# Splitting a 16-chunk product of two norms and a projection 2, 4, 4, 6 instead of 4, 4, 4, 4

## The reference, cut to what matters

```python
mod = jax.nn.silu(c) @ w_mod + b_mod             # c: (1, 2048), w_mod: (2048, 3 * 2048)
shift, scale, gate = jnp.split(mod, 3, axis=-1)
h = rms_norm(x, g_pre) * (1.0 + scale[:, None, :]) + shift[:, None, :]
proj = h @ w_in                                  # (256, 2048) @ (2048, 5648)
...                                              # three mixers on slices of proj
y = jnp.concatenate([y_a, y_b, y_c], axis=-1) * jax.nn.silu(z)   # z: the last 2048 columns of proj
out = y @ w_out
return x + gate[:, None, :] * rms_norm(out, g_post)
```

## Time and profile before

| | |
|---|---|
| median of 3 runs | 2877.43 us (2876.9 to 2878.89) |
| the profiled execution, its own time | 2878.37 us |
| its span, first to last instruction | 2876.2 us |
| PE busy | 2807.3 us, 98% |
| DVE busy | 2162.3 us, 75% |
| ACT busy | 1518.5 us, 53% |
| DMA | 610.86 MB, mean 212 GB/s |

### The profile page before, as it was taken

One profiled execution on the slowest core, in us unless ns is written; L12 is line 12 of the kernel. 1 busy time (PEld: TensorE's weight loads), 2 busy tenths in 40 slices (PEclk: granted clock), 3 DMA queues, 4 the chain that ended last, 5 costly groups with the idle time before them and its releaser, 6 DMA issues.

```text
span 2876.2 us, 37268 instructions
## 1 busy us (share of the span) xinstructions
PE 2807.3 (98%) x14486; PEld 2416.6 (84%) x14486; DVE 2162.3 (75%) x2679; ACT 1518.5 (53%) x2108; POOL 42.7 (1%) x49
## 2 busy tenths in 40 slices
PE   7998998999999999999999999999999999999998
PEld 5886777898889888888888888898888888888887
DVE  8998998678855567666886678745676668866788
ACT  5455544665546555644554455565546445544554
POOL 0000000000000000000000000000000000000000
PEclk9999999999999999999999999999999999999999
DMA  9996597767745554555665566565545565555564
GB/s 394 369 373 227 184 361 301 273 205 249 247 157 174 162 169 154 172 189 195 199 205 183 191 197 199 188 191 162 169 154 172 188 196 199 205 183 191 197 214 160
DMA packets 173744, 610.86 MB, mean 212 GB/s; under 512 B 19665, under 2 KB 19937, under 8 KB 173057
## 3 DMA queue, kind: packets, MB, share of 16 engines
q1 hardware_dynamic: 170770, 599.38, 61.0%
q0 software_dynamic: 1824, 6.61, 0.8%
q10 hardware_dynamic: 976, 2.51, 0.3%
HBM read 606.30 MB, written 2.11 MB: 212 GB/s over the span
## 4 chain that ended last, share of the span: by engine, by line
PE 81%; DVE 3%; ACT 2%; issue 1%; DMA 1%; POOL 0%; SPq 0%; DVEq 0%; POOLq 0%; ACTq 0%
PE ps L2348 16%; PE ps L2279 15%; PE ps L2282 15%; PE ps L2286 14%; PE ps L2358 8%; PE ps L2221 2%; PE ps L2325 1%; PE ps L2327 1%; PE ps L2322 1%; PE ps L2558 1%; PE ps L2331 1%; PE ps L2336 1%; PE ps L2334 1%; DVE w_lo L1414 1%; DMA raw<-in_w_in 1%
## 5 line engine op out<-in xcount | busy, mean ns | idle before, releaser
L1414 DVE TENSOR_TENSOR w_lo<-raw,w_hi 128x1024 fp32r<-128x1024 f32 (+3 forms) x942 | 1088.8, 1176 | 505.2 <-ACT w_hi L1008 501.2
L1008 ACT ACTIVATE w_hi<-raw 128x1024 fp32r<-128x1024 f32 (+3 forms) x942 | 948.1, 1019 | 984.4 <-PE ps L2358 355.0
L2348 PE MATMUL ps<-hT_both,w_hi 128*128 128x512 f32 x2048 | 490.5, 391 | 1.1 <-DVE u L1570 0.9
L2279 PE MATMUL ps<-w_hi,hT_both 128*128 128x512 f32 (+3 forms) x1824 | 479.5, 384 | 7.9 <-DVE proj L1616 2.6
L2286 PE MATMUL ps<-w_hi,hT_both 128*128 128x512 f32 (+3 forms) x1824 | 458.9, 373 | 0.0
L2348 PEld LDWEIGHTS ps<-hT_both,w_hi 128*128 128x128 f32 x2048 | 376.0, 188 | 75.1 <-DVE u L1570 1.3
L2282 PE MATMUL ps<-w_lo,hT_both 128*128 128x512 f32 (+3 forms) x1640 | 414.7, 374 | 3.2 <-DVE w_lo L1414 3.2
L2286 PEld LDWEIGHTS ps<-w_hi,hT_both 128*128 128x128 f32 x1824 | 338.2, 188 | 48.6
L2279 PEld LDWEIGHTS ps<-w_hi,hT_both 128*128 128x128 f32 x1824 | 327.5, 190 | 54.6 <-DVE proj L1616 6.5
L2282 PEld LDWEIGHTS ps<-w_lo,hT_both 128*128 128x128 f32 x1640 | 305.0, 189 | 48.5 <-DVE w_lo L1414 5.0
L2358 PEld LDWEIGHTS ps<-hT_both,w_lo 128*128 128x128 f32 x2048 | 262.8, 191 | 10.2
(11 more groups left out here) (309 smaller groups left out, 2627.2 us busy)
## 6 DMA issues: line engine op xcount, KB each, us to landing
raw<-in_w_up SPq DMA_DIRECT2D x256, 512.0 KB, 3.7
raw<-in_w_down SPq DMA_DIRECT2D x256, 512.0 KB, 3.5
raw<-in_w_modT SPq DMA_DIRECT2D x162, 512.0 KB, 6.8
raw<-in_w_rest SPq DMA_DIRECT2D x80, 456.0 KB, 3.4
raw<-in_w_z SPq DMA_DIRECT2D x54, 512.0 KB, 4.3
raw<-in_w_out SPq DMA_DIRECT2D x49, 512.0 KB, 4.3
raw<-in_w_oa SPq DMA_DIRECT2D x32, 512.0 KB, 3.4
raw_more<-in_w_modT SPq DMA_DIRECT2D x30, 512.0 KB, 6.8
```

Of the source, the lines that this page charges most:

```text
L1008: act.activation(hi_blocks(L % SPLIT_SLOTS, c, w), blocks(raw_at(G), c, w), ACT.Copy).then_inc(S.hi_ready, 1)
L1414: dve.tensor_tensor(blocks(lo_at(G), c, w), blocks(raw_at(G), c, w), hi_blocks(s, c, w).bitcast(F32), ALU.subtract).then_inc(S.group_read, 1)
L2279: pe.matmul(o, rows(hi, c, t), wh[:, c], start=start and c == 0, stop=False)
L2348: pe.matmul(ps[:, bank(job, i, f)], wh[:, c, f * P:(f + 1) * P], hT_both[:, k0 + c].rearrange("p a n -> p (a n)"), start=k0 + c == 0, stop ...
```

## The change

The contraction of layer 0's input product is cut into parts of 2, 4, 4 and 6 chunks instead of four of 4. Layer 1 keeps one product with modulation columns in quarters. What follows from it:

- A has 8 steps (one group to a tile), B and C 16, D 24 (three groups to a tile). The sum stays 64 steps.
- 8 rows (4 pairs) are multiplied ahead of step 0 instead of 16. The 16 rows of B lie over the first 6 steps of A, the 16 of C over the first 13 of B, the 24 of D over the first 13 of C, and the 14 of the gate over the 24 steps of D.
- A has one lead, at step 0. B's two leads stand at steps 6 and 7, C's two at 22 and 23, D's three at 37, 38 and 39.
- DVE's add of a finished tile in D, the rotation and POOL's small loads are placed by steps that fit the longer D.

```diff
-QUARTERS = 4
-QC = KC // QUARTERS
+PORTIONS = (((0, 2), (2, 4), (6, 4), (10, 6)), ((0, 4), (4, 4), (8, 4), (12, 4)))
+FIRST_INPUT = ("ina", "inb", "inc", "ind")
...
-    for q in range(QUARTERS):
-        yield f"in{'abcd'[q]}0", "w_in", 0, q * QC, QC, 0, C_Z, C_Z // 8
+    for kind, (k0, cnt) in zip(FIRST_INPUT, PORTIONS[0]):
+        yield f"{kind}0", "w_in", 0, k0, cnt, 0, C_Z, C_Z // 8
...
-        mods_first = [mod_group(*m) for m in quarter_mods(0, 0)]
-        mods = [m for q in range(1, QUARTERS) for m in quarter_mods(0, q)] + gate_mods(0)
+        def portion_mods(l, q):
+
+            k0, cnt = PORTIONS[l][q]
+            return [(l, part * KC + k, h) for k in range(k0, k0 + cnt) for part in range(2) for h in range(2)]
+        mods_first = [mod_group(*m) for m in portion_mods(0, 0)]
+        mods = [m for q in range(1, len(PORTIONS[0])) for m in portion_mods(0, q)] + gate_mods(0)
...
-        parts = [(product(f"in{'abcd'[q]}0", hT, lhs0=q * QC, evac="dve" if q else "act", pinned=True),
-                  pace_pairs(16, 13) if q < QUARTERS - 1 else pace_pairs(14, 16)) for q in range(QUARTERS)]
+        parts = [(product(f"{kind}0", hT, lhs0=k0, evac="dve" if k0 else "act", pinned=True), times)
+                 for kind, (k0, _), times in zip(FIRST_INPUT, PORTIONS[0], (
+                     pace_pairs(16, 6), pace_pairs(16, 13), pace_pairs(24, 13), pace_pairs(14, 24)))]
...
-        lead("ina0", *after("ina0", 0), first=1)
...
-        for q, name in enumerate(("inb0", "inc0", "ind0")):
-            lead(name, *after(name, -2, -1), first=2 * q + 2)
+        for kind, (k0, cnt) in zip(FIRST_INPUT[1:], PORTIONS[0][1:]):
+            lead(f"{kind}0", *after(f"{kind}0", *range(-(cnt // 2), 0)), first=k0 // 2)
...
-                    walk.upto(jobs["ind0"].L + 9)
+                    walk.upto(last_in.L + 12)
                     rotation = rotation1(l)
                     next(rotation)
-                    walk.upto(jobs["ind0"].L + 11)
+                    walk.upto(last_in.L + 14)
```

More of the change, by code:

```diff
@@ L550, in build, with portion_of, portion_ends @@
         hT = (hT_hi, hT_lo)
-        def quarter_mods(l, q):
-            return [(l, part * KC + q * QC + k, h) for k in range(QC) for part in range(2) for h in range(2)]
+        def portion_mods(l, q):
+            k0, cnt = PORTIONS[l][q]
+            return [(l, part * KC + k, h) for k in range(k0, k0 + cnt) for part in range(2) for h in range(2)]
+        def portion_of(l, k):
+            return next(q for q, (k0, cnt) in enumerate(PORTIONS[l]) if k0 <= k < k0 + cnt)
+        def portion_ends(l, block):
+            return any(block == KC + k0 + cnt - 1 for k0, cnt in PORTIONS[l])
         def gate_mods(l):
             return [(l, 2 * KC + k, h) for k in range(KC) for h in range(2)]
-        mods_first = [mod_group(*m) for m in quarter_mods(0, 0)]
-        mods = [m for q in range(1, QUARTERS) for m in quarter_mods(0, q)] + gate_mods(0)
-        mods += [m for q in range(QUARTERS) for m in quarter_mods(1, q)] + gate_mods(1)
+        mods_first = [mod_group(*m) for m in portion_mods(0, 0)]
+        mods = [m for q in range(1, len(PORTIONS[0])) for m in portion_mods(0, q)] + gate_mods(0)
+        mods += [m for q in range(len(PORTIONS[1])) for m in portion_mods(1, q)] + gate_mods(1)
         shapes = {name: shape for name, *shape in weight_products()}
@@ L943, in _ @@
             rsqrt(2)
-            pool.wait_ge(S.group_multiplied, jobs["ind0"].L)
+            pool.wait_ge(S.group_multiplied, last_in.L + 8)
             for dst, src in ((cst[:, CONST_FIRST:], io["const"][:, CONST_FIRST:]), (cols2[:], io["cols2"]),
@@ L1068, in split_bank @@
                 if layer is not None:
-                    act.wait_ge(S.hcol_ready, QUARTERS * layer + 2 * b // QC + 1)
+                    act.wait_ge(S.hcol_ready, layer * len(PORTIONS[0]) + portion_of(layer, 2 * b) + 1)
                 u = n(S.lhs_hi) - 1
@@ L1163, in split @@
                 l = job.layer
-                if job.kind in ("ina", "inb", "inc", "ind", "in"):
+                if job.kind in (*FIRST_INPUT, "in"):
                     split_bank(hT_hi, b, hcol, mod[:, l], l)
@@ L1182, in wide @@
                 for job, i, j, L, splits in ahead(order):
-                    if prev and prev[0].kind == "ina" and j == 1:
+                    if prev and prev[0].kind == FIRST_INPUT[0] and j == len(job.groups[:2]) - 1:
                         evacuate(*prev)
@@ L1302, in mixers1 @@
                 if l == 0:
-                    d = jobs["ind0"]
+                    d = last_in
                     act.wait_ge(S.dve_evacuated, d.E + 6)
@@ L1611, in evacuate @@
                     return
-                if job.kind in ("inb", "inc", "ind"):
+                if job.kind in FIRST_INPUT[1:]:
                     if job.kind == "inb":
@@ L1646, in mod_product @@
                                          accum_out=mod_part[:, l, block, part:part + 1]).then_inc(S.group_read, 1)
-                if KC <= block < 2 * KC and block % QC == QC - 1 and part:
+                if part and portion_ends(l, block):
                     dve.wait_ge(S.group_read, G + 1)
-                    quarter_columns(l, (block - KC) // QC)
+                    portion_columns(l, block - KC)
             def mod_pair(l, block, part, G):
@@ L1658, in mod_pair @@
                                          accum_out=mod_part[:, l, block, 0:1]).then_inc(S.group_read, 2)
-                if KC <= block < 2 * KC and block % QC == QC - 1:
+                if portion_ends(l, block):
                     dve.wait_ge(S.group_read, G + 2)
-                    quarter_columns(l, (block - KC) // QC)
+                    portion_columns(l, block - KC)
             def side_by_side(G):
@@ L1675, in mod_products, with portion_columns @@
                         mod_product(*second)
-            def quarter_columns(l, q):
-                two = lambda v: v.rearrange("p (s k) -> p s k", s=2)[:, :, q * QC:(q + 1) * QC]
+            def portion_columns(l, last):
+                k0, cnt = PORTIONS[l][portion_of(l, last)]
+                k = slice(k0, k0 + cnt)
+                two = lambda v: v.rearrange("p (s k) -> p s k", s=2)[:, :, k]
                 m = two(mod[:, l, 0:2 * KC])
@@ L1683, in quarter_columns @@
                 link(dve.tensor_tensor(m, m, two(cols1[:, l, 16:16 + 2 * KC]), ALU.add))
-                k = slice(q * QC, (q + 1) * QC)
                 dve.scalar_tensor_tensor(out=hcol[:, k], in0=m[:, 1], scalar=1.0, in1=cols1[:, l, k],
@@ L1703, in wide @@
                         evacuate(*ended.pop(0)[0:2])
-                    if prev and prev[0].kind in ("inb", "inc", "ind") and j == 1:
+                    if prev and prev[0].kind in FIRST_INPUT[1:] and j == 1:
                         evacuate(*prev)
@@ L1879, in rotation1 @@
                 else:
-                    dve.wait_ge(S.dve_evacuated, jobs["ind0"].E + 3)
+                    dve.wait_ge(S.dve_evacuated, last_in.E + 3)
                 heads = QH + KVH
@@ L2266, in group_product @@
                 if pinned(job, i):
-                    start, stop = start and job.kind == "ina", stop and job.kind == "ind"
+                    start, stop = start and job.kind == FIRST_INPUT[0], stop and job.kind == FIRST_INPUT[-1]
                 terms = [(c, t, ps[:, bank(job, i, t), 0:job.width]) for c in range(cnt) for t in tokens]
@@ L2580, in gla @@
                 else:
-                    pe.wait_ge(S.dve_evacuated, jobs["ind0"].E + 7)
+                    pe.wait_ge(S.dve_evacuated, last_in.E + 7)
                 transposes([proj[:, t, C_CG:C_CG + RANK] for t in range(TOK)], RANK)
```

1 line of the change is left out of this document (added).

## The result

| | before | after |
|---|---|---|
| median | 2877.04 us (13 runs, 2875.02 to 2878.89) | 2884.02 us (13 runs, 2882.54 to 2888.27) |
| profiled execution, its span | 2876.2 us | 2882.2 us |
| time over that of before | | 1.0025, 95% interval 1.0017 to 1.0034 |

The change costs 6.98 us on the median; the forecast was 2884.4, 7.0 above its median. In the changed kernel `lo` is L1424, the pair L1666, the add L1626, the columns L1694 to L1696, the lead's subtraction L1768, and the three terms of a product L2290, L2293 and L2297.

What follows compares the result with a forecast made beforehand. DVE was taken to bound the kernel up to D's columns, PE behind them; D's end 7.3 us later less 0.3 past D gave 7.0 on the median 2877.43, 2884.4 us, range 2877.5 to 2890.

Steps and rivals of the forecast that it cites:

- The opening: Up to step 0's product: A's columns at 23.2, first product at 28.6 instead of 35.35, 6.7 us earlier.
- What the early start is worth: From 22.6 to D's columns: DVE idles 3.3 us instead of 5.7, a gain of 2.4 us.
- D's columns: The point where DVE forms D's columns, which fixes D: at 144.8 instead of 155.86.
- D: Last part, 24 steps: bound by PE at 2.44 us a product, takes 66.3 us, ends at 211.1, 7.3 us later.
- Past D: Behind D's end: DVE is less late for the first maxima, 0.3 of 1.1 us regained.
- the saving on DVE: Ahead of D's columns: 8 `lo` and one lead fewer on DVE, 8.1 and 0.6 us.
- PE is the bound: Rival, whole stage: PE keeps the 6.7 us of its earlier start, 2870.7 us, faster; chance 0.09.
- Given back past D: Rival, behind D: DVE's spare time in D absorbs the 7 us, 2877.4 give or take 2; chance 0.15.
- DMA doesn't keep up in C: Rival, C's loads: at 366 GB/s they take 50.8 instead of 45.2 us, 5.6 more, 2890; chance 0.08.
- TensorE's clock falls: Rival, C: PE's waits bring the low clock, 16 products take 68 us instead of 52, 2900; chance 0.05.
- The waits in C: PE's waits between products in C: 0.8 to 1.8 us each, held against the clock falling.
- the signs that I had named for being wrong: D's columns before 138, D's end before 205, C at clock 0.5, landing idle in A or C, shorter stretch past D.

Runs made afterwards that it cites:

- late_start: The changed kernel with 8 pairs ahead of step 0, as before, in place of 4: 2885.2 us, 1.0028 to the kernel before.
- no_gate_rows: The changed kernel with the 14 gate rows in D neither loaded nor multiplied: 2884.63 us, 1.0027 to the kernel before.
- more_dve_d: The changed kernel with two more DVE reductions of 2048 elements, 2.2 us each, in D: 2885.34 us, 1.0030 to the kernel before.
- more_dve_c: The changed kernel with two more DVE reductions of 2048 elements, 2.2 us each, in C: 2889.32 us, 1.0042 to the kernel before.
- narrow_multiply: The changed kernel with D's 24 modulation rows loaded in full but multiplied over 64 columns only: 2884.99 us, 1.0030 to the kernel before.
- split_4426: The changed kernel cut into parts of 4, 4, 2 and 6 chunks, with the start of the kernel before: 2894.11 us, 1.0059 to the kernel before.

## Why the prediction was right, and where it was not

*The opening.* A's columns at 23.01 (23.2 forecast), the first `lo` at 26.84 (26.8), the first product at 28.57 (28.6): right, and so was the list of what stands between.

*What the early start is worth* was the term that was mis-sized. I gave it 2.4 us of DVE's idle time. DVE idled 4.84 us up to D's columns (2.02, 0.48, 2.24 and 0.10 by the windows) instead of 3.3, against 5.86 before: a gain of 1.0. And late_start has the same 4.8 us of idle time without the early start, so the start earns none of it. Of the 1.5 us that I missed, 1.2 are at B's leads: 2.1 us (0.43, 1.02, 0.54 and 0.15) instead of the 0.9 of my estimate. The kernel before shows nearly the same waits at the same place, 2.0 us (0.30, 1.02, 0.54 and 0.16), and there PE has the full clock (1.00 up to 77.62). So half clock (below) is not what costs them, and I could have read the term from DVE's timeline of the kernel before:

```profile
73.42 0.69 DVE L1757 TENSOR_TENSOR hT_both<-hf,hT_both 128x512 fp32r<-128x512 f32 x1 [0.30 <-ACT hT_both L1086]
75.14 1.10 DVE L1414 TENSOR_TENSOR w_lo<-raw,w_hi 128x900 fp32r<-128x900 f32 x1 [1.02 <-ACT w_hi L1008]
76.77 0.69 DVE L1757 TENSOR_TENSOR hT_both<-hf,hT_both 128x512 fp32r<-128x512 f32 x1 [0.54 <-ACT hT_both L1086]
```

*D's columns* at 145.5 instead of 144.8. DVE's busy time up to them fell by 9.28 us (127.40 to 118.12 over the windows), where 8 `lo` and a lead made 8.7; with the 1.0 of idle time that is 10.3 instead of 11.1.

*D* took 66.10 us (66.3 forecast) and PE idled 0.21 in it. This is the term that decides, and no_gate_rows and more_dve_d show from both sides that it is PE's.

*Past D* the first maxima lost 0.2 of the 7.8 (0.3 forecast), and nothing was given back. Sum: 7.6 behind the first maxima on the trace, 7.0 on the median. The mechanism was right, but that the median met the forecast of 7.0 to a tenth is luck: the gain from the early start was set 1.4 too high and the saving on DVE 0.6 too low, and the interval of the measured ratio (1.0017 to 1.0034) runs from 4.9 to 9.8 us.

*PE is the bound* fell with late_start and more_dve_c. *Given back past D* fell with the earlier trace rows and their counterparts above.

*DMA doesn't keep up in C* did not happen, but was near: the loads bind at 48.1 us where DVE takes 51.5 and I had counted 44.8 against 45.2 for 13 steps. The queue held 417 to 418 GB/s for the 29 us from 22.60 to 51.83 and 418 in C of narrow_multiply. The Trainium skill, "DMA: Bandwidth & Descriptors", section "Specifications", gives some 358 GB/s for a core, the 716 of a stack halved between two cores. The trace differs here too, with one core at work.

*TensorE's clock falls* did happen, in two places, and cost little. The windows of the changed kernel, at B's start and in C:

```profile
54.00:58.00 4.00, 4.00 (x12) 3.54 (x11) 2.10 (x3) 3.91 (x8) 0.00 (x0) 0.50 1.03 415
...
118.00:120.00 2.00, 2.00 (x12) 1.85 (x11) 2.00 (x3) 0.29 (x1) 0.00 (x0) 1.00 1.02 383
...
134.00:136.00 2.00, 2.00 (x6) 1.78 (x6) 2.00 (x4) 0.95 (x1) 0.00 (x0) 0.50 1.02 415
```

and PE's timeline at B's start, then at three of the waits for an add in C:

```profile
51.03 1.29 PE L2290 MATMUL ps<-w_hi,hT_both 128*128 128x450 f32 x4 [2.05 <-ACT w_hi L1018]
...
54.64 1.70 PE L2297 MATMUL ps<-w_hi,hT_both 128*128 128x450 f32 x4
...
117.34 1.08 PE L2290 MATMUL ps<-w_hi,hT_both 128*128 128x450 f32 x4 [2.29 <-DVE proj L1626]
118.26 0.98 PE L2293 MATMUL ps<-w_lo,hT_both 128*128 128x450 f32 x4
...
124.78 1.07 PE L2290 MATMUL ps<-w_hi,hT_both 128*128 128x450 f32 x4 [2.29 <-DVE proj L1626]
...
132.22 1.07 PE L2290 MATMUL ps<-w_hi,hT_both 128*128 128x450 f32 x4 [2.29 <-DVE proj L1626]
...
134.17 1.70 PE L2297 MATMUL ps<-w_hi,hT_both 128*128 128x450 f32 x4
```

The waits in C are longer than I had them (0.8 to 1.8 us), since PE does two steps in one go and then stands 2.29 us for the add that frees the PSUM bank. Behind the waits that end at 117.34 and 124.78 the granted clock stayed at 1.00, which is 2.4 GHz (windows 118 to 120 and 124 to 129); behind the one that ends at 132.22 it fell to 0.50, 1.2 GHz (134 to 136). The slow products in C cost nothing that the rows show: DVE, which sets C, has no gap there. At B's start DVE's waits are 0.1 us longer than at full clock in the kernel before. The rule that I weighed, of the Trainium skill, "TensorE: Matmul & The Clock Gate", section "HAM oscillation — how this bites in real kernels", has every burst of such a loop start at the low clock. The trace agrees for the waits of 5.63, 5.46 and 3.74 us in split_4426 and for one of these three of 2.29 us, not for every burst. The 2900 of that rival needed every product of C at half clock. Two of the signs that I had named for being wrong did show, then, each small: products in C at a clock of 0.5, and 0.21 us in which DVE waits for a landing ahead of A's last pair (at 49.01; 48.8 forecast).

## What to carry to other kernels

When a product's operand is computed by another engine, split the time at the moment when the last part of the operand is ready: ahead of it the producer's list counts, behind it the products left over, at TensorE's own pace. A larger last part leaves more products behind that moment and earns nothing ahead of it if the producer is already full; a smaller first part starts the products earlier and earns nothing either. Before moving work off the engine that binds, measure the limits behind it (here loads 3 us behind DVE at D's columns, 1.3 at D's end), and whether the idle engine can work beside it at all.

## What was not expected of the hardware

- A GpSimd subtraction of 128x900 (1.95 to 2.6 us in all but one case) held up the DVE instruction that was due next by about 1.76 us when that had two operands in SBUF: pairs went from 2.28 to 4.04 us. It was held up in turn by one already under way: it took 3.82 us where a pair had 2.00 us left to run, 2.45 where a `lo` had 0.63 left, and 1.96 beside an add that had 0.58 left.
- The granted clock fell to half behind waits of 2.05 and 2.29 us in this loop, and did not behind two others of 2.29.
- One core's loads ran at 417 to 418 GB/s for 29 us on end.
